# Context rows of V added on TensorE instead of VectorE, in a mixer and expert kernel with its units unrolled

## The reference, cut to what matters

```python
def peer(h, wq, keys, u_tab, v_tab):
    q = (x @ wq).reshape(T, PEER_HEADS, 2, PEER_HALF)
    s = jnp.einsum('thpd,hpnd->thpn', q, keys)
    s_top, i_top = lax.top_k(s, 16)                     # 16 of 128 keys, twice
    cand = s_top[:, :, 0, :, None] + s_top[:, :, 1, None, :]
    sc, pos = lax.top_k(cand.reshape(T, 8, 256), 16)    # 16 of 256 pairs
    gate = jax.nn.softmax(sc, axis=-1)
    ...
        ue = jnp.take(u_tab, it, axis=0)                # 128 rows of U per token
        ve = jnp.take(v_tab, it, axis=0)                # 128 rows of V per token
        a = jax.nn.gelu(jnp.einsum('td,ted->te', xt, ue))
        return jnp.einsum('te,ted->td', gt * a, ve)
```

## Time and profile before

| | |
|---|---|
| time, median of two runs | 4652.51 us (4648.87 and 4656.16) |
| span of the profiled execution | 4627.7 us, 24.8 us less than the median |
| time of the profiled execution as a run | not recorded apart from the two runs |
| PE busy | 3424.7 us (74%), 9648 matmul records |
| DVE busy | 2972.4 us (64%) |
| POOL busy | 2880.2 us (62%), 2560 row fetches |
| ACT busy | 1072.4 us (23%) |
| DMA | 1486.11 MB, mean 321 GB/s |
| granted TensorE clock, mean | 0.935 |

### The profile page before, as it was taken

How to read it: one execution, slowest core, us unless ns; L and a number is a source line. 1 busy time by engine, 2 the same in 40 slices (tenths; PEclk the granted TensorE clock), 3 DMA queues, 4 the chain that set the end, 5 groups by cost and what they waited for, 6 DMA issues and landing times.

```text
span 4627.7 us, 39193 instructions
## 1 busy us (share of the span) xinstructions
PE 3424.7 (74%) x9648; PEld 1527.8 (33%) x9648; DVE 2972.4 (64%) x6847; ACT 1072.4 (23%) x2261; POOL 2880.2 (62%) x2564
## 2 busy tenths in 40 slices
PE   8778886678778776677676978946666766667777
PEld 2644653122333332222222546422222222222222
DVE  0279999545566555666664889986666665656662
ACT  1332321121232212121122323211212112121222
POOL 0034555456667676777773545657777777777775
PEclk9889898899999899999998989969999999999999
DMA  7468788989899998999995977879999999999998
GB/s 286 162 224 294 256 298 284 351 314 360 332 354 353 335 370 323 360 376 346 354 377 170 331 257 249 328 258 354 361 355 339 356 360 333 363 341 346 371 370 295
DMA packets 392139, 1486.11 MB, mean 321 GB/s; under 512 B 44108, under 2 KB 45838, under 8 KB 375888
## 3 DMA queue, kind: packets, MB, share of 16 engines
q0 software_dynamic: 368640, 1342.34, 79.5%
q1 hardware_dynamic: 23248, 141.13, 8.0%
HBM read 1480.42 MB, written 2.88 MB: 321 GB/s over the span
## 4 chain that ended last, share of the span: by engine, by line
DMA 32%; PE 25%; DVE 17%; issue 17%; POOL 6%; ACT 3%; POOLq 0%; SPq 0%; DVEq 0%; ACTq 0%
DMA rows_ring<-in_peer_v,idx 19%; DMA rows_ring<-in_peer_u,idx 12%; PE psum L825 12%; POOL rows_ring L548 6%; DVE rows_ring L1366 5%; DVE mix L1380 4%; PE psum L648 4%; PE psum L604 3%; PE psum L770 1%; PE psum L635 1%; DVE small L1288 1%; DMA ring<-in_ada 1%; PE psum L782 1%; PE psum L811 0%; PE psum L597 0%
## 5 line engine op out<-in xcount | busy, mean ns | idle before, releaser
L825 PE MATMUL psum<-rows_ring,diag 128*128 128x512 f32 x4096 | 2067.1, 634 | 901.0 <-DMA rows_ring<-in_peer_v,idx 723.9
L1366 DVE SCALAR_TENSOR_TENSOR rows_ring<-rows_ring,area 128x1024 f32<-128x1024 f32 x1280 | 1562.7, 1225 | 957.9 <-DMA rows_ring<-in_peer_u,idx 935.2
L548 POOL DMA_INDIRECT rows_ring<-in_peer_u,idx x1280 | 1419.7, 1109 | 1084.5 <-DVE rows_ring L1366 431.9
L548 POOL DMA_INDIRECT rows_ring<-in_peer_v,idx x1280 | 1460.3, 1141 | 637.4 <-issue 287.1
L825 PEld LDWEIGHTS psum<-rows_ring,diag 128*128 128x128 f32 x4096 | 730.6, 196 | 2192.0 <-issue 950.6
L1057 ACT ACTIVATE diag<-ident,wts 128x128 f32<-128x128 f32 x1024 | 381.7, 397 | 1515.1 <-PE psum L825 1514.3
L648 PE MATMUL psum<-area,ring 128*128 128x128 f32 (+1 forms) x1344 | 381.8, 443 | 17.1 <-ACT area L919 17.1
L1380 DVE SCALAR_TENSOR_TENSOR mix<-rows_ring,wts,mix 128x1024 f32<-128x1024 f32 x254 | 326.2, 1284 | 8.7 <-DMA rows_ring<-in_peer_v,idx 7.6
L648 PEld LDWEIGHTS psum<-area,ring 128*128 128x128 f32 x1344 | 213.4, 198 | 188.2 <-issue 185.1
L604 PE MATMUL psum<-ring,csil 128*2 128x512 f32 x384 | 176.4, 615 | 21.5 <-DMA ring<-in_ada 21.5
L1049 ACT ACTIVATE acts<-dots 128x16 f32<-128x16 f32 x80 | 17.3, 216 | 555.8 <-DVE rows_ring L1366 555.6
(11 more groups left out here) (174 smaller groups left out, 2473.6 us busy)
## 6 DMA issues: line engine op xcount, KB each, us to landing
ring<-in_ada SPq DMA_DIRECT2D x48, 1024.0 KB, 7.1
ring<-in_win SPq DMA_DIRECT2D x32, 1024.0 KB, 7.7
rows_ring<-in_peer_u,idx POOLq DMA_INDIRECT x1280, 6.1
rows_ring<-in_peer_v,idx POOLq DMA_INDIRECT x1280, 6.2
ring<-in_wout SPq DMA_DIRECT2D x16, 1024.0 KB, 6.7
ring<-in_wq SPq DMA_DIRECT2D x16, 1024.0 KB, 7.3
ring<-in_dft SPq DMA_DIRECT2D x12, 1024.0 KB, 7.7
xT<-in_xT_in SPq DMA_DIRECT2D x1, 2560.0 KB, 15.2
```

Of the source, the lines that this page charges most:

```text
L548: pool.indirect_dma_start(row(table, k), None, (peer_u, peer_v)[table], bass.IndirectOffsetOnAxis(ap=idx[n][:, k:k + 1], axis=0)).then_inc ...
L825: m = pe.matmul(acc[:, b, :], diag[:, k % 4, :], row(1, k)[:, b * 512:(b + 1) * 512], start=False, stop=False)
L1366: dve.scalar_tensor_tensor(out=row(0, k), in0=row(0, k), scalar=1.0, in1=h_tok[GROUPS[grp][1]][:, bass.ds(t * D_MODEL, D_MODEL)], op0=ALU. ...
```

## The change

Context rows of V are added like the latent ones, on PE with a diagonal from ACT; the DVE adds of line 1380 are gone, and a context tile is closed like a latent one. All hardware loops and both tick semaphores are gone, and every engine walks the list unrolled. Rows go in quads: POOL issues four rows of U, then four of V; a step does four dots, then four adds, and V is now one and a half units behind U (quads 2 and 3 of unit u - 2, then quads 0 and 1 of unit u - 1). A tile is closed after its last quad (`close`, in the second quarter of a step), DVE adds it to the tokens after the next four dots (`added`), and PE opens the next tile's sum after that. `pick` reads the scores where they are, without `stage`. The weights of a unit have four places. The mixer's jobs take five banks (3 to 7) instead of six. Attention has two pairs of banks instead of three, its scores are one unit ahead instead of two, and its output has one bank.

```diff
 def attention_jobs(l, st):
-    jobs = [("fence", l, st, 0), ("as", l, st, 0), ("as", l, st, 1)]
+    jobs = [("fence", l, st, 0), ("as", l, st, 0)]
     for n in range(n_units):
-        jobs += [("as", l, st, n + 2)] if n + 2 < n_units else []
+        jobs += [("as", l, st, n + 1)] if n + 1 < n_units else []
...
+PICK_AT = ((0, 1), (2,), (3, 4), (5,))
+QUADS = TOPK // 4
 def step_jobs(grp, u):
-    jobs += [("open", grp, u - 1, 0)] if u % PEER_HEADS == 1 else []
-    jobs += [("stage", grp, u + 1, 0)] if u + 1 < n else []
-    for p in range(PIECES):
+    for p in range(QUADS):
         jobs += [("dot", grp, u, p)] if u < n else []
-        jobs += [("add", grp, u - 1, p)] if u else []
-        jobs += [("pick", grp, u + 1, p // 2)] if u + 1 < n and p % 2 and p // 2 < PICK_PARTS else []
+        if p == 2 and u >= PEER_HEADS + 1 and u % PEER_HEADS == 1:
+            jobs += [("added", grp, u - 2, 0)]
+        if p == 2 and u >= 1 and (u - 1) % PEER_HEADS == 0 and u <= n:
+            jobs += [("open", grp, u - 1, 0)]
+        m, g = (u - 2, p + 2) if p < 2 else (u - 1, p - 2)
+        if 0 <= m < n:
+            jobs += [("add", grp, m, g)]
+        if p == 1 and u >= PEER_HEADS + 1 and u % PEER_HEADS == 1:
+            jobs += [("close", grp, u - 2, 0)]
+        if u + 1 < n:
+            jobs += [("pick", grp, u + 1, part) for part in PICK_AT[p]]
     jobs += [("weigh", grp, u, 0)] if u < n else []
     jobs += [("gexp", grp, u + 1, 0)] if u + 1 < n else []
-    jobs += [("close", grp, u - 1, 0)] if u and u % PEER_HEADS == 0 else []
...
-BANK = {j: 2 + i % 6 for i, j in enumerate(BANKED)}
+BANK0, BANKS = 3, 5
+BANK = {j: BANK0 + i % BANKS for i, j in enumerate(BANKED)}
...
         def att_bank(st, n):
-            return psum_cols[:, 1024 * (1 + n % 3):1024 * (2 + n % 3)]
+            at = 512 * (BANK0 + 2 * (n % 2))
+            return psum_cols[:, at:at + TOK]
...
         def _(pool):
-            def fetch(table, grp, u, n, k):
-                pool.wait_ge(s[("u_free", "v_free")[table]], (u + UNIT0[grp]) * TOPK + k + 1)
-                pool.sem_inc(s["pool_tick"], 1)
-                pool.indirect_dma_start(row(table, k), None, (peer_u, peer_v)[table],
+            def fetch_u(v, p):
+                for k in range(4 * p, 4 * p + 4):
+                    if v * TOPK + k >= ROWS:
+                        pool.wait_ge(s["u_free"], v * TOPK + k + 1 - ROWS)
+                    pool.indirect_dma_start(row(0, k), None, peer_u,
...
+            for job in ORDER:
+                kind, grp, u, p = job
+                if kind == "dot":
+                    if p == 0:
+                        pool.wait_ge(s["idx_ready"], u + UNIT0[grp] + 1)
+                    fetch_u(u + UNIT0[grp], p)
+                elif kind == "add":
+                    fetch_v(u + UNIT0[grp], p)
...
             def att_scores(l, st, n):
-                if n >= 3:
-                    pe.wait_ge(s["pt_ready"], done("at", l, st, n - 3))
+                if n >= 2:
+                    pe.wait_ge(s["pt_ready"], done("at", l, st, n - 2))
...
+            def add(v, g):
+                for k in range(4 * g, 4 * g + 4):
+                    pe.wait_ge(s["diag_ready"], v * TOPK + k + 1)
+                    pe.wait_ge(row_landed[1][k % ROWS], row_value(v, k))
                     for b in range(2):
                         m = pe.matmul(acc[:, b, :], diag[:, k % 4, :], row(1, k)[:, b * 512:(b + 1) * 512], start=False, stop=False)
                     m.then_inc(s["v_free"], 1)
...
                 elif kind == "at":
                     att_copy(a, b, n)
-                    if n + 2 < ATT_UNITS[b]:
-                        att_exp(a, b, n + 2)
+                    if n + 1 < ATT_UNITS[b]:
+                        att_exp(a, b, n + 1)
...
-            def add(g, u, p):
-                for k in range(PER_PIECE * p, PER_PIECE * (p + 1)):
-                    dve.wait_ge(row_landed[1][k % ROWS], row_value(g, k))
-                        m = dve.scalar_tensor_tensor(out=out_tok[C_], in0=x, scalar=wts[:, k:k + 1], in1=out_tok[C_],
-                                                     op0=ALU.mult, op1=ALU.add)
-                    m.then_inc(s["v_free"], 1)
...
                 elif kind == "as":
-                    att_max(a, b, n)
                     if n:
                         att_norm(a, b, n - 1)
+                    att_max(a, b, n)
```

## The result

The changed kernel takes 5181.5 us (median of two runs, 5171.78 and 5191.22) against 4652.51 us: 1.1157 times as long, 95% interval 1.112 to 1.1193. It is slower, as forecast; the time is 226 us above the predicted one and 31 us above the end of the range. The profiled execution spans 5170.0 us against 4627.7, so 542 us are to be explained.

What follows compares the result with a forecast made beforehand. DVE, narrowly ahead of PE, was taken to bound the woven stages and POOL the latent ones. 362 - 36 - 43 + 13 + 7 = +303 us on 4652.5 gave 4955 us, 6.5% slower, range 4790 to 5150.

Steps and rivals of the forecast that it cites:

- PE takes over as the bound, and the stage cannot hide it: Woven stages: moved adds give PE 220 us more, 692 us in all against a stage of 570; DVE falls to 341.
- the forecast's lower bound, +122: Per woven stage: PE's 692 us of work against 570, with no stall at all; the upper bound was +248.
- The reading of 0.43 us from start to start as occupancy: PE's records start 0.43 us apart, taken as occupancy, not pipeline tails: 1.72 us a row, 220 us for 128 rows.
- +362 for the woven stages: Twice +181 a stage: +35 before attention, +65 in it, +81 behind it, for layer 0 and again for layer 1.
- The waits that the change adds ... ask for things that are done earlier in the same list: New waits on DVE (gelu before the next dots, V used before an index place is written) were priced at nothing.
- Tile ends, -36: Latent tile ends: no loop turn, POOL keeps rows out; six ends save 6 us each, bounds 0 and -44.
- POOL's pace, -43: Latent-only stretches: dropping the tick's semaphore instruction saves 0.03 us on each of 1441 fetches; bounds 0 to -312.
- The second rival: Latent stages: POOL's 0.30 us gap shrinks much, DMA reaches 415 GB/s, -312 instead of -43, 4686 us; chance 0.10 for most.
- Quads not slowing POOL: Four dots in a row on DVE could hold POOL's fetches longer; taken as no change.
- POOL paces these stages: Latent stages: POOL issues a fetch every 1.48 us, 1.145 busy and 0.30 gap, with DMA hardly behind.
- The third rival, the clock: Latent stages: PE idles between quads, clock falls, +360, 5315 us; signs: clock under 0.9, POOL waiting for PE; chance 0.08.
- the small terms: Terms outside the woven stages: tile ends -36, POOL's pace -43, heads and tails +13, closing context tiles +7.

Runs made afterwards that it cites:

- experiment 5: The changed kernel with rows one at a time and context adds back on DVE, new banks and unrolled list kept: 4644.32 us, ratio 1.0024 to before.
- 9: The changed kernel, quads kept, with context adds back on DVE and `pick` parts earlier: 4771.03 us, ratio 1.0287 to before.
- experiment 7: The changed kernel with the parts of `pick` behind quads 0, 0, 1, 1, 2, 2 instead of 0, 0, 1, 2, 2, 3: 5032.45 us, ratio 1.0868 to before.
- after: The changed kernel with the whole change in it, against the kernel before: 5181.5 us, ratio 1.1157.
- before: The kernel without the change: 4652.51 us timed beside after, 4635 to 4641 us beside the experiments.
- 3: The changed kernel with rows one at a time, a part of `pick` after each second row, adds still on PE: 5145.47 us, ratio 1.1102 to before.
- 13: As 8, but ACT makes the latent rows' diagonals two rows ahead, in six places instead of four: 4595.11 us, ratio 0.991 to before.
- experiment 11: As 3 (single rows, adds on PE), but ACT makes diagonals two rows ahead, in six places instead of four: 4848.06 us, ratio 1.0446 to before.
- experiment 2: The kernel before with only the new banks and attention order (scores one unit ahead, five mixer banks): 4669.04 us, ratio 1.0077.
- 8: As experiment 5, but attention on three banks, scores two units ahead and six mixer banks as before: 4632.36 us, ratio 0.9987 to before.

## Why the prediction was right in its direction and wrong in its size

Experiments 5, 9, 7 and after form a chain in which each differs from the last by one part of the change, so the whole difference can be read by stage (us, on the grid of 10):

| | woven 0 | latent 1 | woven 1 | latent 2 | sum |
|---|---|---|---|---|---|
| all the rest (before to 5) | +30 | -10 | +20 | -30 | +10 |
| quads (5 to 9) | +40 | +30 | +40 | +20 | +130 |
| adds moved to PE (9 to 7) | +130 | +20 | +130 | -20 | +260 |
| `pick` late (7 to after) | +30 | +40 | +20 | +50 | +140 |
| all | +230 | +80 | +210 | +20 | +540 |

The sum does not depend on the order in which the parts come; the prices of the adds and the quads do. In single rows the moved adds cost 501 us (5 to 3), because each then waits for its diagonal, and 253 us with the diagonals ahead (13 to 11). And quads, which cost 127 us beside adds on DVE (5 to 9), gain 113 us beside adds on PE (3 to 7). Only the late `pick` was measured as one edit on the changed kernel itself.

**"PE takes over as the bound, and the stage cannot hide it": right.** Line 1380 is gone, DVE is at 45%, PE at 87%. The moved adds cost +130 a stage in quads, and 130 again in single rows once the diagonals come in time (11 against 13). That is the forecast's lower bound, +122. The reading of 0.43 us from start to start as occupancy held: PE's busy time came out at 697.66 us against 692. That it is so close is in part luck, since busy time also holds the records at the lower clock; in experiment 11 it is 670 us. Weight loads are busy for 374 of 798 us, and for 359 of the 708 of experiment 11, where nothing but PE is left. The rule from the Trainium skill, Perfetto Trace Analysis, section Identifying the Most-Contended Engine, read by the share of weight loads (47% and 51%), would have left both stages room on TensorE. The page names that share together with MFU, the share of the peak arithmetic rate, which was not worked out here. The measurements decide against the share of weight loads for this kind of fp32 product.

**+362 for the woven stages: too small by 82 us.** Here the mechanism was right and the stall mis-sized: the forecast added some 59 us a stage to PE's 692, put down to attention and small losses, and measured are 106 (798 less 692). By the chain it is not one stall: quads cost 40 there with the adds still on DVE, the late `pick` 20 to 30, and banks and lag 20 to 30. Attention took 230 us where 215 were forecast. The banks alone make 20 of its 80 (experiment 2). The remainder comes with the quads, the late `pick` and the waits for diagonals. How it divides between the blocks of four dots on DVE and the blocks of 6.9 us on PE was not separated.

**"The waits that the change adds ... ask for things that are done earlier in the same list": this step failed.** It looked at the waits that are new in the code. The costly one is old: POOL's wait for `idx`. Its words did not change, the place of what it waits for did, from after row 11 to after row 15, and that move had no line in the sum. It cost about 140 us (experiment 7), where the result lies 31 us outside the range. The rows to price it were there, in the trace of before, where DVE does the last part ahead of the dot of row 12:

```profile
3471.60 0.42 DVE L1352 TENSOR_TENSOR onehot<-tok_const,posf 128x256 f32<-128x256 f32 x1
...
3473.18 0.17 DVE L1359 TENSOR_SCALAR idx<-idxf 128x16 uint32<-128x16 f32 x1
...
3473.72 1.23 DVE L1366 SCALAR_TENSOR_TENSOR rows_ring<-rows_ring,area 128x1024 f32<-128x1024 f32 x1 [0.37 <-DMA rows_ring<-in_peer_u,idx]
```

It takes 1.75 us (3471.60 to 3473.35), and as long behind the last dot in the trace after (4105.03 to 4106.78). 64 latent units give 112 us if nothing covers it; by the chain the two latent stages lost 90. In the trace of before no wait for `idx` stands in a latent stage, which should have been read as slack that an edit could use up.

**Tile ends, -36, and POOL's pace, -43.** Experiment 5 has -40 us in the latent stages, less than the 66 forecast and of the same sign. The traces do not show them where the forecast put them. The loop turn is gone, but the stand of POOL behind a tile's end is not. At the three ends inside the last stage POOL stood for 7.3, 8.1 and 3.4 us before; it stands for 6.6, 9.2 and 8.1 us in experiment 5 and for 4.4, 3.3 and 4.5 us after. It now waits for PE. Two of these places, first in experiment 5, then after, each with PE's opening of the next sum:

```profile
3910.59 3.78 PE L787 MATMUL psum<-cos_sin,zeros 128*128 128x512 f32 x4 [2.25 <-DVE xT L1333]
3917.59 1.35 POOL L528 DMA_INDIRECT rows_ring<-in_peer_v,idx  x1 [9.20 <-PE psum L795]
```

```profile
4048.65 3.02 PE L782 MATMUL psum<-cos_sin,zeros 128*128 128x512 f32 x4 [3.10 <-DVE xT L1313]
4054.32 1.96 POOL L525 DMA_INDIRECT rows_ring<-in_peer_v,idx  x1 [4.44 <-PE psum L790]
```

The forecast had taken that opening at 1.7 us at full clock, inside the slack of four fetches. It stands behind an idle piece of PE again, at a granted clock of 0.50 (3910.6 to 3914.4 us of experiment 5) and 0.64 (4048.6 to 4051.7 us of after). So -36 is not shown.

For the pace the reason was wrong. The gap of 0.30 us is there without the tick's instruction, as the timeline of after shows at full load:

```profile
4108.29 0.94 POOL L516 DMA_INDIRECT rows_ring<-in_peer_u,idx  x1 [0.30 <-issue]
...
4109.53 0.94 POOL L516 DMA_INDIRECT rows_ring<-in_peer_u,idx  x1 [0.30 <-issue]
```

The second rival rested on this gap and falls with it. In the last stage of experiment 5 a fetch does start every 1300 / 900 = 1.44 us, where from 3200 to 4500 us of before it was 1300 / 876 = 1.48:

```profile
3200.00:4500.00 1300.00, 906.20 (x1844) 319.29 (x1844) 828.87 (x2046) 258.57 (x592) 1002.10 (x900) 0.98 0.97 363
```

That is the size that the forecast took, by luck: each fetch holds POOL for 1.11 us instead of 1.15. In the latent-only part of layer 0 both kernels are at 1.45 us, so there nothing was gained.

**"Quads not slowing POOL": right, and more.** From 3700 to 5050 us, groups by line of the kernel after:

```profile
L525 POOL DMA_INDIRECT rows_ring<-in_peer_v,idx x456 | 543.3, 1192 | 190.4 <-issue 99.1 <-PE psum L790 88.7 <-DVE rows_ring L1294 2.6
L516 POOL DMA_INDIRECT rows_ring<-in_peer_u,idx x456 | 433.2, 950 | 184.3 <-issue 130.8 <-DVE idx L1284 52.9 <-DVE rows_ring L1294 0.6
```

A fetch holds POOL for 976.5 / 912 = 1.07 us, where it was 1.145, and still one starts every 1350 / 912 = 1.48 us. POOL got faster and the pace did not: waits for PE and `idx` took the place. So "POOL paces these stages" was half true. Without the late `pick` the same fetches come at 1.44 us (624 in 900 us of experiment 7), as in experiment 5, at 363 GB/s and a DMA share of 0.97:

```profile
4000.00:4900.00 900.00, 659.06 (x1280) 268.30 (x1280) 583.73 (x1426) 185.26 (x409) 661.35 (x624) 0.87 0.97 363
```

The Trainium skill, SBUF — State Buffer, section SBUF: two separate sides, has an exclusive port between a DVE op with two SBUF inputs and a GpSimd op that reads SBUF; the one that starts first blocks the other. The traces agree in one direction: over the whole of after, the 891 fetches that start inside a dot take 1.33 us on average and the others 0.94. The other direction does not show: the 678 dots of after that start well inside a fetch take 1.22 us like all others. That bunching dots must hold more fetches does not follow; fetches of U fell to 0.95 us from 1.10. In the last stage of before 174 of 490 of them started inside a dot and took 1.40 us; from 3700 to 5050 us of after it is 71 of 455 and 1.01 us. They now start mostly while DVE waits for their rows.

**The third rival, the clock.** It fell as that rival says, to 0.85 to 0.87, and its other sign came too, POOL waiting for PE (117.8 us in the last stage; before it was 100.3). Behind an idle piece like this one the granted clock is 0.50 (4118 to 4121 us) and the records take twice the time, then it is back:

```profile
4118.14 7.30 PE L790 MATMUL psum<-rows_ring,diag 128*128 128x512 f32 x13 [5.36 <-DMA rows_ring<-in_peer_v,idx]
...
4119.12 0.34 PEld L790 LDWEIGHTS psum<-rows_ring,diag 128*128 128x128 f32 x1 [0.52 <-issue]
...
4121.85 0.19 PEld L790 LDWEIGHTS psum<-rows_ring,diag 128*128 128x128 f32 x1 [0.24 <-issue]
```

Its price, +360, did not come: a stage at 0.87 (experiment 7) is as short as one at 0.97 (13), 1510 us both. The two differ in more than the clock, so a small price could hide. PE is busy for 1073 of 1510 us there, which leaves room for the slow starts.

**What made up the miss.** Against the forecast: moved adds +260 where PE's floor gives +244; stalls in the woven stages beyond its allowance +66; latent stages +164 (from -66 to +98), of which the late `pick` is 90 and the quads are 50. The range's upper end held +496 for the woven stages, more than they took; what it had no room for was a loss in the latent ones. (With the small terms as they stand in the sum, the two bounds come to some 4840 and 5090 us; 4790 and 5150 leave more room than the working shows.) Without the late `pick` the time is that of experiment 7, 5032 us, inside the range.

## What to carry to other kernels

When a regrouping changes an order that all engines share, list the last producer before each unit's first consumer and count what lies between them before and after; a wait that is absent from the trace is slack, and an edit can spend it. When work moves to an engine that is already four-fifths busy, take its start-to-start times as occupancy, and the floor of the stage is their sum; then ask who makes its operands, and let that engine run a few items ahead in a ring of its own. That was worth 297 us of 5145 here with single rows, and 37 us of 4632 with the adds left where they were (8 to 13).

## What the runs showed that was not expected

- POOL's 0.30 us between two indirect fetches does not depend on a semaphore instruction between them: it reads 0.30 with one and without.
- Single rows and quads change places by what else is late. With diagonals made just in time, quads with the early `pick` win in the woven stages (764 and 780 us against 844 and 870) and lose in the first latent one (1720 against 1660). With diagonals ahead, single rows win in the first three stages (714, 1630, 730 against 734, 1710, 740) and the last is equal, 1520 us.
- The stand of POOL behind a latent tile's end outlived the loop turn that it had been put down to: it was 9.2 us at one end of experiment 5, which has no loop.
- A granted clock lower by 0.1 in a stage bound by fetches cost no time that shows (experiments 7 and 13).
